# A block of a transformer in float32 on one core: rows of the rounded input padded to 576 columns, and the arena of the other tiles moved within its 256-byte lines

## The reference

```
def hybrid_layer(h, ...):
    xn = rms_norm(h, norm1_g)
    p = xn @ w_in
    (u_pool, q, c_lat, q_idx, k_idx, w_idx, cb, cc, cu, g_raw) = split_columns(p)
    y_a = pool_mixer(u_pool, pool_w, pool_scale) @ w_a
    attn = dsa_attention(...)
    y_b = attn @ w_b
    y_c = short_conv_mixer(cb, cc, cu, conv_w) @ w_c
    g = jax.nn.sigmoid(g_raw + b_gate).reshape(B, L, N_BRANCH, D_MODEL)
    h = h + (g[:, :, 0] * y_a + g[:, :, 1] * y_b + g[:, :, 2] * y_c) @ w_o
    gate, up = jnp.split(rms_norm(h, norm2_g) @ w_gate_up, 2, axis=-1)
    return h + (jax.nn.silu(gate) * up) @ w_down
...
def second_block(x, p, ...):
    x = x + 0.5 * swiglu(rms_norm_2(x, ffn1_norm[i]), ...)          # 1024 -> 2816 -> 1024
    h = rms_norm_2(x, mix_norm[i])
    fq, fk, fv, f_logit, sq, sk, sv, g_fox, g_sb = split_columns_2(h @ w_in[i])
    y_fox = forgetting_attention(...)      # logits use a running sum of log forget gates
    y_sb = stick_breaking_attention(...)
    x = x + merged @ w_out[i]
    x = x + 0.5 * swiglu(rms_norm_2(x, ffn2_norm[i]), ...)
    x = x + jax.nn.sigmoid(rms_norm_2(x, ple_norm[i]) @ w_ple_gate[i]) * (p[i] @ w_ple_proj[i])
```

## The kernel before

| moving operand | columns | before | after |
|---|---|---|---|
| `xh`, `xl`, steps k = 0 to 7 | 512 | 192, 0, 64, 128, and again | 128 in every step |
| `xh`, `xl`, both halves with the meta columns | 264 | 128 + 64k and 160 + 64k | 64 and 96 |
| `fh`, `fl` of feed-forward 0 / 1 / 2 | 512 | 32 / 32 / 32 | 128 / 0 / 64 |
| `ath`, `atl`, `mh`, `ml`, `ah`, `al`, `coh`, `col_` | 512 | 96 | 128 |
| `m2h`, `m2l`, `yfh`, `yfl`, `ysh`, `ysl`, `pTh`, `pTl` | 512 | 32 | 128 |
| `whi`, `wlo` (weights) | 128 or 256 | 128 | 128 |

## Time and profile before

### The profile page before, as it was taken

One profiled execution on the slowest core, in us unless ns is written; L12 is line 12 of the kernel. 1 busy time (PEld: TensorE's weight loads), 2 busy tenths in 40 slices (PEclk: granted clock), 3 DMA queues, 4 the chain that ended last, 5 costly groups with the idle time before them and its releaser, 6 DMA issues.

```text
span 2127.2 us, 26554 instructions
## 1 busy us (share of the span) xinstructions
PE 2086.8 (98%) x9561; PEld 1674.4 (79%) x9561; DVE 886.4 (42%) x1394; ACT 754.5 (35%) x1038; POOL 1002.3 (47%) x754
## 2 busy tenths in 40 slices
PE   8999999999999999999999999998899999999999
PEld 7798886678888888788888887886667888888877
DVE  6787735534333321343333124465654533332124
ACT  6412224434222222332222234666654432222222
POOL 5344442145555554455555445544434455554543
PEclk9999999999999999999999999999999999999999
DMA  4222231123333323233332232111122333332232
GB/s 154 75 89 92 88 99 60 40 70 88 99 99 99 90 84 108 86 88 98 99 99 88 95 94 80 57 48 57 40 70 89 99 99 85 92 99 94 89 104 80
DMA packets 250057, 184.01 MB, mean 87 GB/s; under 512 B 7040, under 2 KB 247168, under 8 KB 249984
## 3 DMA queue, kind: packets, MB, share of 16 engines
q1 hardware_dynamic: 249296, 182.74, 28.5%
q10 hardware_dynamic: 688, 0.31, 0.1%
HBM read 180.93 MB, written 2.10 MB: 86 GB/s over the span
## 4 chain that ended last, share of the span: by engine, by line
PE 91%; DVE 4%; POOL 2%; ACT 2%; issue 1%; DMA 0%; SPq 0%; DVEq 0%; ACTq 0%; POOLq 0%
PE ps L543 28%; PE ps L544 28%; PE ps L545 28%; POOL wlo L451 1%; DVE sc L1433 1%; PE ps L764 1%; PE ps L749 1%; PE ps L907 1%; PE ps L830 1%; PE ps L831 1%; PE ps L832 1%; DVE ssum L1561 0%; DVE pu L1934 0%; PE ps L757 0%; PE ps L763 0%
## 5 line engine op out<-in xcount | busy, mean ns | idle before, releaser
L451 POOL TENSOR_TENSOR wlo<-raw,whi 128x512 fp32r<-128x512 f32 (+1 forms) x692 | 940.6, 1391 | 1007.4 <-ACT whi L1003 953.6
L543 PE MATMUL ps<-xh,whi 128*128 128x512 f32 (+2 forms) x1912 | 741.6, 388 | 12.9 <-DVE xl L1433 7.4
L544 PE MATMUL ps<-xl,whi 128*128 128x512 f32 (+2 forms) x1912 | 733.0, 383 | 0.0
L545 PE MATMUL ps<-xh,wlo 128*128 128x512 f32 (+2 forms) x1912 | 729.6, 382 | 0.0
L1003 ACT ACTIVATE whi<-raw 128x2048 fp32r<-128x2048 f32 (+1 forms) x159 | 297.6, 1872 | 827.6 <-PE ps L545 825.1
L543 PEld LDWEIGHTS ps<-xh,whi 128*128 128x128 f32 (+1 forms) x1912 | 359.9, 188 | 91.7 <-issue 11.7
L545 PEld LDWEIGHTS ps<-xh,wlo 128*128 128x128 f32 (+1 forms) x1912 | 359.4, 188 | 73.0
L544 PEld LDWEIGHTS ps<-xl,whi 128*128 128x128 f32 (+1 forms) x1912 | 359.3, 188 | 71.1 <-issue 2.5
L1487 DVE TENSOR_TENSOR tmp<-ps,rs 128x512 f32<-128x512 f32 x148 | 102.1, 692 | 341.8 <-PE ps L545 324.6
L544 PE MATMUL ps<-fl,whi 128*128 128x512 f32 x528 | 209.4, 397 | 0.0
L545 PE MATMUL ps<-fh,wlo 128*128 128x512 f32 x528 | 209.4, 397 | 0.0
(11 more groups left out here) (297 smaller groups left out, 2185.2 us busy)
## 6 DMA issues: line engine op xcount, KB each, us to landing
raw<-in_w_in SPq DMA_DIRECT2D x90, 512.0 KB, 4.6
raw<-in_w_gate_up SPq DMA_DIRECT2D x44, 512.0 KB, 4.8
raw<-in_ffn_w_gate SPq DMA_DIRECT2D x44, 512.0 KB, 4.0
raw<-in_ffn_w_up SPq DMA_DIRECT2D x44, 512.0 KB, 5.2
raw<-in_ffn_w_down SPq DMA_DIRECT2D x32, 512.0 KB, 3.9
raw<-in_w_down SPq DMA_DIRECT2D x16, 512.0 KB, 4.0
raw<-in_ffn_w_down SPq DMA_DIRECT2D x16, 384.0 KB, 3.4
raw<-in_w_b SPq DMA_DIRECT2D x8, 512.0 KB, 3.9
```

The costliest lines, as they stand in the source:

```text
L451: ins = pool.tensor_tensor(wlo[:, c % 2, cs], raw[:, c % 2, cs], whi[:, c % 2, cs].bitcast(F32), ALU.subtract)
L543: pe.matmul(o, w_of(whi), xhi, start=first, stop=False)
L544: pe.matmul(o, w_of(whi), xlo, start=False, stop=False)
L545: return pe.matmul(o, w_of(wlo), xhi, start=False, stop=last)
```

## The change

`xh` and `xl` get rows of 576 columns (2,304 bytes, nine lines of 256), of which 528 are used as before. `vec`, `eps`, `m8` and other small tensors are allocated elsewhere, so that the arena starts 128 bytes into a line (before: 32), and the offsets inside it are shifted by 48 words for the first layer's operands. The hidden values of the three feed-forwards get an address each (`F_AT`, in words). To make room, the running sum of the forget gates no longer reads a tensor of ones (`fone`), and `sk11` takes the place of constants no longer used by then.

```diff
+ROW = 576
+F_AT = (0, 32, 48)
...
-        xh = sb("xh", [P, DK, TM], F32R)
-        xl = sb("xl", [P, DK, TM], F32R)
+        vec = sb("vec", [P, V_ROWS + DK])
+        xh = sb("xh", [P, DK, ROW], F32R)
+        xl = sb("xl", [P, DK, ROW], F32R)
...
-        arena_cols = 28160
-        pad = sb("pad", [P, (-((nc.sbuf_base + 31) // 32 * 32) % 256 + 28) // 4])
+        arena_cols = 27648
+        pad = sb("pad", [P, (128 - (nc.sbuf_base + 31) // 32 * 32) % 256 // 4 or 64])
...
-        fh = at("fh", 0, [P, FK, T], F32R)
-        fl = at("fl", FK * T, [P, FK, T], F32R)
-        tmp = at("tmp", 2 * FK * T, [P, 4, T])
+        fh = [at(f"fh{f}", o, [P, FK, T], F32R) for f, o in enumerate(F_AT)]
+        fl = [at(f"fl{f}", FK * T + o, [P, FK, T], F32R) for f, o in enumerate(F_AT)]
+        tmp = at("tmp", 2 * FK * T + 64, [P, 4, T])
...
-        ath = at("ath", 1168, [P, HEADS, T], F32R)
+        ath = at("ath", 1216, [P, HEADS, T], F32R)
...
-            pool.memset(fone[:], 1.0).then_inc(consts, 1)
...
-            dve.tensor_tensor_scan(fF[:], fone[:], fz[:], 0.0, ALU.mult, ALU.add).then_inc(f_done, 1)
+            dve.tensor_tensor_scan(fF[:], fz[:], fz[:], 0.0, ALU.add, ALU.bypass).then_inc(f_done, 1)
```

More of the change, by code:

```diff
@@ L111, in build @@
         hT = sb("hT", [P, DK, TM])
-        xh = sb("xh", [P, DK, TM], F32R)
-        xl = sb("xl", [P, DK, TM], F32R)
+        vec = sb("vec", [P, V_ROWS + DK])
+        xh = sb("xh", [P, DK, ROW], F32R)
+        xl = sb("xl", [P, DK, ROW], F32R)
+        eps = sb("eps", [P, 1])
+        m8 = sb("m8", [P, 8])
         raw = sb("raw", [P, 2, CH])
@@ L121, in build @@
         ssum = sb("ssum", [P, TM])
-        vec = sb("vec", [P, V_ROWS + DK])
         ident = sb("ident", [P, P])
@@ L125, in build @@
         ones = sb("ones", [P, P])
+        causalr = sb("causalr", [P, P], F32R)
+        strictr = sb("strictr", [P, P], F32R)
+        first_start = (nc.sbuf_base + 31) // 32 * 32
         onesblk = sb("onesblk", [P, P])
         causal = sb("causal", [P, P])
-        causalr = sb("causalr", [P, P], F32R)
         strict = sb("strict", [P, P])
-        strictr = sb("strictr", [P, P], F32R)
-        eps = sb("eps", [P, 1])
         wi = sb("wi", [P, QB, HEADS])
+        rest = sb("rest", [P, 3 * HEADS * QB])
         nmx = sb("nmx", [P, QB * HEADS])
@@ L135, in build @@
         rden = sb("rden", [P, QB * HEADS])
-        m8 = sb("m8", [P, 8])
         rtok = sb("rtok", [P, QB])
         fbias = sb("fbias", [8, 1])
-        arena_cols = 28160
-        pad = sb("pad", [P, (-((nc.sbuf_base + 31) // 32 * 32) % 256 + 28) // 4])
+        arena_cols = 27648
+        pad = sb("pad", [P, (128 - (nc.sbuf_base + 31) // 32 * 32) % 256 // 4 or 64])
         start = (nc.sbuf_base + 31) // 32 * 32
@@ L159, in build @@
         ctok = at("ctok", 528, [P, QB + 1, P])
-        qT = at("qT", 1168, [P, HEADS, T])
-        ath = at("ath", 1168, [P, HEADS, T], F32R)
[L162 to L191, removed]
+        qT = at("qT", 1216, [P, HEADS, T])
+        ath = at("ath", 1216, [P, HEADS, T], F32R)
@@ new lines, in build @@
+        sc = at("sc", 5312, [P, QB, TM])
+        ah = at("ah", 7424, [P, 4, T], F32R)
+        al = at("al", 9472, [P, 4, T], F32R)
+        coh = at("coh", 11520, [P, 4, T], F32R)
+        col_ = at("col_", 13568, [P, 4, T], F32R)
+        cl = at("cl", 15616, [P, TM])
+        kw = at("kw", 16144, [KW, TM])
+        qst = at("qst", 7424, [3 * D_IDX, HEADS, T], F32R)
+        kst = at("kst", 11520, [3 * D_IDX, TM], F32R)
+        qih = at("qih", 12048, [P, 2, T], F32R)
+        qiT = at("qiT", 17200, [P, 2, T])
@@ new lines, in build @@
+        rl = at("rl", 18224, [P, 2, TM])
+        rc = at("rc", 19280, [P, TM])
+        u = at("u", 19808, [P, 4, TM])
+        pooled = at("pooled", 15616, [P, 4, T])
+        win = at("win", 17664, [P, 2, TM])
+        cc = at("cc", 18720, [P, 4, TM])
+        cv = [at("cv0", 20832, [P, TM])[:], at("cv1", 24432, [P, TM])[:]]
+        cy = at("cy", 21360, [P, 4, T])
+        pwt = at("pwt", 23408, [P, 4, P])
+        co = at("co", 23920, [P, T])
+        msum = at("msum", 15616, [P, DK, T])
+        atl = at("atl", 7424, [P, HEADS, T], F32R)
@@ L193, in build @@
+        pT = at("pT", 11520, [P, QB + 1, T])
+        lm = at("lm", 14080, [P, 2, TM])
+        pr = at("pr", 23808, [P, 2, TM])
+        gb = at("gb", 19712, [P, DK, T])
+        mh = at("mh", 11520, [P, DK, T], F32R)
+        ml = at("ml", 15616, [P, DK, T], F32R)
         qF = at("qF", 0, [P, 4, T])
@@ L217, in build @@
         fFs = at("fFs", 27136, [8, T], F32R)
-        fone = at("fone", 27648, [8, T])
         sq1 = [at(f"sq1{z}", 25600 + 1536 * z, [P, T], F32R) for z in range(2)]
-        sk1 = [at(f"sk1{z}", 26112 + 1536 * z, [P, T], F32R) for z in range(2)]
+        sk1 = [at("sk10", 26112, [P, T], F32R), nc.alloc_sbuf_tensor_at("sk11", [P, T], F32R, offset=first_start)]
         sk2 = [at("sk20", 26624, [P, T], F32R), nc.alloc_sbuf_tensor_at("sk21", [P, T], F32R, offset=ssum_start)]
@@ L475, in _ @@
             pool.memset(sel[:], 0.0).then_inc(consts, 1)
-            pool.memset(fone[:], 1.0).then_inc(consts, 1)
             for z in range(2):
-                pool.wait_ge(consts, 11 + z)
+                pool.wait_ge(consts, 10 + z)
                 pool.memset(kt2[z][far(z), :].bitcast(F32), 0.0).then_inc(consts, 1)
             for z, first in enumerate((0, 32, 64, 96)):
-                pool.wait_ge(consts, 13 + z)
+                pool.wait_ge(consts, 12 + z)
                 pool.affine_select(out=sel[:], in_=sel[:], compare_op=ALU.not_equal, fill=1.0, base=-first,
@@ L637, in ffn @@
                                     mm = passes(ps[:, bank(c + j, t), :], cr % 2, lambda wt: wt[:, cr % 2, o:o + P],
-                                                fh[:, k0 + k, :], fl[:, k0 + k, :], r == 0 and k == 0, r == 2 and k == kn - 1)
+                                                fh[f][:, k0 + k, :], fl[f][:, k0 + k, :], r == 0 and k == 0, r == 2 and k == kn - 1)
                                 mm.then_inc(tile_done, 1)
@@ L1046, in up @@
                     act.wait_ge(h_done, lin(FK * f + n + 1, per, i))
-                    act.activation(one(fh, lin(n, per, i)), tmp[:, 3, :], ACT.Copy).then_inc(h_hi, 1)
+                    act.activation(one(fh[f], lin(n, per, i)), tmp[:, 3, :], ACT.Copy).then_inc(h_hi, 1)
                 root(S)
@@ L1259, in _ @@
             act.activation(fFs[:], fF[:], ACT.Copy).then_inc(f_hi, 1)
-            act.wait_ge(consts, 17)
+            act.wait_ge(consts, 16)
             for z in range(2):
@@ L1514, in ffn @@
                         nn = lin(j, 2, i)
-                        dve.tensor_tensor(one(fl, nn), tmp[:, 3, :], one(fh, nn).bitcast(F32), ALU.subtract).then_inc(h_split, 1)
+                        dve.tensor_tensor(one(fl[f], nn), tmp[:, 3, :], one(fh[f], nn).bitcast(F32), ALU.subtract).then_inc(h_split, 1)
                         dve.wait_ge(h_split, lin(n + 1, 2, i))
@@ L1831, in _ @@
             link(stt(fz[:], fz[:], 0.0, ft[:], ALU.min, ALU.subtract))
-            dve.wait_ge(consts, 13)
-            dve.tensor_tensor_scan(fF[:], fone[:], fz[:], 0.0, ALU.mult, ALU.add).then_inc(f_done, 1)
+            dve.wait_ge(consts, 12)
+            dve.tensor_tensor_scan(fF[:], fz[:], fz[:], 0.0, ALU.add, ALU.bypass).then_inc(f_done, 1)
             dve.wait_ge(f_done, 1)
```

## The result

| | before | after |
|---|---|---|
| median | 2130.06 us (4 runs, 2128.17 to 2130.72) | 2096.87 us (4 runs, 2096.56 to 2097.18) |
| ratio | | 0.9846, 95% interval 0.9829 to 0.9863 |
| span of the profiled execution | 2127.2 us | 2095.4 us |

A forecast was written before the change was run, and what follows sets the result against it. TensorE's streaming was taken to bound the kernel, its matmul pace set by where moving rows start. Terms -8.6 (`xh`/`xl`), -5.0 (`fh`/`fl`), -3.8 (other arena), +1.3 (waits) summed to -16.1 us: 2113.4 us, range 2105 to 2123.5.

The forecast's parts named there:

- the extra sequencer instruction: Ahead of `xl`, an added register step of the loops: forecast hidden, at most 0.4 us.
- Rival D: All matmuls: the start has no effect, paces differ by something else; 2129 us, chance 0.07.
- rival E: `xh` and arena: any constant start costs, so `xh` slows to 233.3 or 234.3 ns; 2137 to 2142 us, chance 0.07.
- the price of 128: Matmuls of 512 columns with moving rows starting 128 bytes into a line: 230.0 ns each, bounds 226.4 and 233.3.
- the term of `xh`: `xh`/`xl` at 128 in every step: 5040 matmuls from 231.7 to 230.0 ns, -8.6 us, bounds -26.7 and +8.1.
- feed-forward 0: Its `fh`/`fl` tiles move from 32 to 128 bytes: 528 matmuls gain 4.3 ns each, -2.3 us.
- the rest of the arena: Other arena tiles, before at 96 or 32 bytes: 576 matmuls x 3.3 and 432 x 4.4 ns, together -3.8 us.
- The price of 57.5 ns per 128 columns: From durations of matmuls of 512, 384 and 256 columns (395, 339, 280 ns): 512 columns take 230 ns.
- rival B: `xh` and arena: 128 is better than its step shows, as neighbours slow it; at 228 ns 2101 us, chance 0.08.
- The price of 0 and 64: `fh`/`fl` of feed-forwards 1 and 2 at these starts: 231.7 ns, -2.7 us, bounds nothing to -4.5.
- Rival C: Only whole 64-byte starts matter: `xh` gains nothing, the arena moves to 231.7 ns; 2123 us, chance 0.12.
- The waits: Where TensorE waits for another engine's chain, faster matmuls ahead only lengthen the wait: +1.3 us given back.

## Why the prediction was wrong

What bounds the kernel, that the start of the moving rows sets the pace, the sign, and that nothing else of the change costs: right. No wait for the fewer fill or for the scan appeared, and the extra sequencer instruction is not to be seen either: the longest wait for `xl` is the first again, 7.4 us. Rival D (no effect of the start) and rival E (a constant start costs) are out; E is half true of starts other than the weights'.

The step that failed is the price of 128: "If it holds for the pace, 128 gives 231.7 - 2.1 = 229.6 ns", "I take **230.0 ns**". In rows of nothing but 128 it measured 226.7. With it the term of `xh` was -25.2 instead of -8.6 us by the paces (-21.2 from start to start), feed-forward 0 -3.9 instead of -2.3, the rest of the arena -6.8 instead of -3.8. Two readings led there.
- I took what a start costs among other starts for what it costs alone. For its place in the mixed family 230.0 ns was right: there the step at 128 has 230.0 from start to start, as its neighbours slow it. That a duration led to this number was luck, as a duration doesn't give a pace: the tiles at 0 and at 160 bytes last 394 and 396 ns in the median and follow one another at 233.3 ns both. The mean of the family would not have shown the pace of 128 safely either. One fast start and three slow ones at 233.3 give 4 x 231.7 - 3 x 233.3 = 226.9 ns, the right number, but the constant paces that were measured later average 230.6 and not 231.7.
- The price of 57.5 ns per 128 columns, which seemed to confirm 230, was again a difference of durations, of eight matmuls a length between others in an attention. An error of 1 ns in it is 4 ns for 512 columns, so it could not tell 226.7 from 230.

I had 226.4 ns as the lower bound of that term, with its -26.7 us, and rival B for it at 0.08, with the mechanism right (128 is better than its step shows, because the neighbours slow it) and too small a size. The bound should have carried more weight than a duration booked next to a 398.

The price of 0 and 64, 231.7 ns, was also taken from the mixed family, and was too low: 233.3, the bound named there, so -1.1 instead of -2.7 us. Rival C was wrong: whole 64-byte starts are not what counts. And the cause as I had it, the start in the line, is only half of it: it is the start against that of the weights.

The waits took 1.1 us against 1.3 forecast. What the forecast lacked is that the 876 `xh`/`xl` matmuls in short groups, counted at the full gain, would gain almost nothing: 0.7 us of the 4.4 that 5.0 ns each would be. That error goes against the other, and hid some of it.

The experiments' best version has all operands' starts equal: 2089.52 us at 128, a single 2089.19 at 0, 7.4 us under the changed kernel.

## What to carry to other kernels

When TensorE streams without waits, read its pace from first and last starts for each tile apart, and compare tiles by where their rows start against where the weights start: here, with 512 moving columns, equal starts within 256 bytes gave 226.7 ns and most others 233.3. That is 2.9% of the pace and, with all tiles at 128, 1.8% of the kernel's time, for a few bytes of padding. With 256 moving columns equal starts were not the best, so measure each shape. Don't take the pace of a start alone from its step in a mixed family, neither from durations nor from the family's mean: the neighbours enter both, and only a run with that start throughout shows it. And vary each side of a coincidence: two operands stood at 128, and only moving each alone told which mattered.

## What the runs showed of the hardware

- With the granted clock of every profiled execution at 0.998 to 1.0 in the mean, the best pace of float32r matmuls of 512 columns was 226.7 ns. At the other paces single intervals differ (229 and 238 ns by turns with `xh` at 0) and repeat after a few matmuls, and the sum of one repeat lies a whole number of 6.67 ns above that of as many at 226.67:

| pace, ns | seen with | repeats after | sum, ns | times 6.67 above |
|---|---|---|---|---|
| 226.7 | equal starts | 1 | 226.7 | 0 |
| 228.9 | all feed-forward tiles at 192 | 3 | 686.7 | 1 |
| 231.7 | `xh` in the kernel before | 12 | 2780 | 9 |
| 232.4 | `xh` with the weights at 0 | 7 | 1626.7 | 6 |
| 233.3 | `xh` at 0 | 2 | 466.7 | 2 |
| 234.3 | `fh` in the kernel before | 7 | 1640.0 | 8 |

6.67 ns is the time of 16 cycles at 2.4 GHz, the upper level of the clock. That the sums come in such units is worked out from these paces; what the unit is, no run shows.
- The starts of the moving and the stationary operand interact: moving only the weights by 128 bytes took `fh` from 226.7 to 232.4 or 233.3 ns, and moving both kept 226.7. The period is 256 bytes: the padded rows put `xh` at alternate halves of 512 bytes and all steps last 389 ns.
- One matmul in three with unequal starts slowed that one only between 260 and 281 us (228.9 ns in the mean), and brought the mean of the three to 233.3 between 560 and 690 us, in two executions alike. Why is open.
- A step's cost depends on its neighbours: the step of `xh` at 128 bytes has 230.0 ns a matmul among starts of 192, 0 and 64, and 226.7 among its like.
